# A two-part transformer kernel: the second part's norm becomes the head of its projection, the context's keys and values are made in the second layer's attention

## The reference, cut to what matters

```
for l in range(2):
    x = x + 0.5 * swiglu(rms_norm(x, norm_ffn1[l]), ffn1_in[l], ffn1_out[l])
    h = rms_norm(x, norm_mix[l]); proj = h @ w_in[l]
    ... o_a = rwkv7_mixer(...); o_b = diff_attention(...)
    x = x + merged @ w_out[l]
    x = x + 0.5 * swiglu(rms_norm(x, norm_ffn2[l]), ffn2_in[l], ffn2_out[l])
```

```
m  = silu(c) @ mod_w[l] + mod_b[l]            # sh1, sc1, g1, sh2, sc2, g2
h  = rms_norm(x, norm1_g[l]) * (1 + sc1) + sh1
mc = silu(c_ctx) @ mod_w[0] + mod_b[0]        # csh1, csc1 are used
hc = rms_norm(ctx, norm1_g[0]) * (1 + csc1) + csh1
q, k, v, ua, va = split(h @ w_in);  kc, vc = split(hc @ w_in[:, 512:768])
x = x + g1 * (concat(window_attention(q, k, v, kc, vc), chunk_gmlp(ua, va)) @ w_out)
x = x + g2 * peer_ffn(norm(x) ...)            # 8 heads x 16 experts for each token
```

## Time and profile before

| | us |
|---|---|
| three runs | 3255.67, 3258.58, 3261.69 |
| median | 3258.58 |
| profiled execution | 3255.88 |
| its span | 3253.7 |
| granted TensorE clock, mean of the span | 0.958 |

### The profile page before, as it was taken

How to read it: one execution, slowest core, us unless ns; L and a number is a source line. 1 busy time by engine, 2 the same in 40 slices (tenths; PEclk the granted TensorE clock), 3 DMA queues, 4 the chain that set the end, 5 groups by cost and what they waited for, 6 DMA issues and landing times. The chain is left out here.

```text
span 3253.7 us, 45326 instructions
## 1 busy us (share of the span) xinstructions
PE 2836.7 (87%) x16786; PEld 1877.1 (58%) x16786; DVE 2139.0 (66%) x3990; ACT 1311.9 (40%) x2973; POOL 581.2 (18%) x516
## 2 busy tenths in 40 slices
PE   7999988799999998879988999997778899777877
PEld 5877676578787877757856665432322555233332
DVE  5755766577575577657734577777775577777764
ACT  4433433344343353144422434444443335444443
POOL 0000000000000000000000025454444045444442
PEclk9999999999999999989987999999999999999999
DMA  7745201387584530137753369999999699999997
GB/s 271 267 165 177 87 3 41 142 276 261 195 276 175 180 113 3 41 112 255 276 200 142 103 275 426 427 426 427 427 427 427 236 418 427 427 427 427 427 427 314
DMA packets 252571, 858.38 MB, mean 264 GB/s; under 512 B 15031, under 2 KB 138807, under 8 KB 179517
## 3 DMA queue, kind: packets, MB, share of 16 engines
q0 software_dynamic: 73728, 536.90, 39.2%
q1 hardware_dynamic: 178622, 318.59, 27.9%
HBM read 847.05 MB, written 8.39 MB: 263 GB/s over the span
## 5 line engine op out<-in xcount | busy, mean ns | idle before, releaser
L3202 POOL DMA_INDIRECT raw_weights<-peer_rows,expert_ids x208 | 237.6, 1142 | 2247.4 <-DVE expert_ids L148 1966.0
L447 PE MATMUL banks<-weight_parts_hi,normedT_hi 128*128 128x512 f32 (+2 forms) x1152 | 458.9, 398 | 38.6 <-DVE weight_parts_lo L1147 12.0
L3312 PE MATMUL banks<-raw_weights,diagonals 128*128 128x512 f32 x832 | 409.6, 636 | 82.0 <-ACT diagonals L181 81.6
L449 PE MATMUL banks<-weight_parts_hi,normedT_lo 128*128 128x512 f32 (+2 forms) x1152 | 448.1, 389 | 0.0
L448 PE MATMUL banks<-weight_parts_lo,normedT_hi 128*128 128x512 f32 (+2 forms) x1152 | 447.9, 389 | 0.0
L3312 PE MATMUL banks<-query_weights,diagonals 128*128 128x512 f32 x704 | 335.9, 618 | 58.3 <-ACT diagonals L181 58.1
L3312 PEld LDWEIGHTS banks<-raw_weights,diagonals 128*128 128x128 f32 x832 | 158.6, 200 | 323.1 <-ACT diagonals L181 165.6
L157 DVE CUSTOM_DVE_ANT_0 modulation<-raw_weights,normed 128x1024 f32<-128x1024 f32 x208 | 255.0, 1226 | 129.3 <-DMA raw_weights<-peer_rows,expert_ids 118.3
L3312 PE MATMUL banks<-modulation,diagonals 128*128 128x512 f32 x512 | 248.6, 623 | 59.2 <-ACT diagonals L181 59.1
L181 ACT ACTIVATE gelu<-dots 128x1 f32<-128x1 f32 x512 | 102.0, 199 | 475.2 <-DVE dots L157 474.5
L157 DVE CUSTOM_DVE_ANT_0 modulation<-query_weights,normed 128x1024 f32<-128x1024 f32 x176 | 215.7, 1226 | 114.5 <-DMA query_weights<-peer_rows,expert_ids 104.9
(11 more groups left out here) (402 smaller groups left out, 4777.7 us busy)
## 6 DMA issues: line engine op xcount, KB each, us to landing
raw_weights<-ffn_in SPq DMA_DIRECT2D x88, 1024.0 KB, 7.5
side_weights<-mod_tiles SPq DMA_DIRECT2D x48, 1024.0 KB, 5.1
raw_weights<-ffn_out SPq DMA_DIRECT2D x44, 1024.0 KB, 6.1
raw_weights<-w_in SPq DMA_DIRECT2D x28, 1024.0 KB, 5.0
query_weights<-peer_w_q SPq DMA_DIRECT2D x16, 1024.0 KB, 10.8
raw_weights<-w_in SPq DMA_DIRECT2D x10, 1536.0 KB, 6.4
raw_weights<-w_branch SPq DMA_DIRECT2D x8, 1024.0 KB, 7.5
raw_weights<-w_out SPq DMA_DIRECT2D x8, 1024.0 KB, 6.3
```

What stands on the lines that cost most here:

```text
L447: nc.tensor.matmul(out, lhs.hi, rhs.hi, start=start, stop=False)
L449: return nc.tensor.matmul(out, lhs.lo, rhs.hi, start=False, stop=stop)
L3202: nc.gpsimd.indirect_dma_start(out=ring.rows(g), out_offset=None, in_=table, in_offset=bass.IndirectOffsetOnAxis(ap=ids[:, n, t:t + 1], ax ...
L3312: last = nc.tensor.matmul(k.bank(2 * j + half), diag[:, g % DIAGS, :], ring.rows(g)[:, D + half * BANK:D + (half + 1) * BANK], start=t == ...
```

## The change

What it does, part by part:

- **Start.** One stage `first_stage` in place of two: conditions first, then x in two halves, gains, only the first 512 columns of the constants, then the weights. ScalarE makes Silu and squares as each lands. The other constants load inside the first feed-forward stage, behind the second side load.
- **Side sums.** Each block's accumulator is loaded with a tile that holds the bias in its first row and zeros elsewhere; all eight products of a block are then multiply-adds. In layer 1 the order of blocks is changed so that those which the norm of the second part needs are ready after its first feed-forward, and its double blocks are 1 and 4 instead of 1 and 7.
- **Context.** `ContextKV` makes the context's keys and values in layer 1 of the first part: squares of the context at the end of the RWKV projection, the root beside the chunk work, then in `finish_mixers` 32 matmuls with two columns of ones that turn the partial sums into columns (4 behind each unit's values), gain and shift folded into columns, the product of the shift, and the product of context and weights; the keep-warm matmuls go. Values use bank 4 alone in this layer. The products are unsplit fp32. The result goes to DRAM.
- **Entry.** The two norm and modulation stages and the context's linear stage go. The projection's first two weight tiles load at the end of the last feed-forward stage, and the norm is the head of the projection (`ShiftedHead`). The partial sums, tables and context keys and values are loaded beside it, ahead of weight tile 2.
- **Row sums.** Eight row sums take the place of eight keep-warm matmuls in `window_mix`, with four copies on ScalarE and four on VectorE, and waits on them.
- **Expert layer.** No bias rows are loaded, no one-row matmuls made.

```diff
+def first_stage(k, a, lam, wts):
+            sp.dma_start(k.cond[:, :], a["cond_columns"]).then_inc(S["got"], 16)
+            for j in range(NT):
+                sp.dma_start(k.X[:, j, :], a["x"][0, j * P:(j + 1) * P, :]).then_inc(S[f"part_in{j}"], 16)
+            sp.dma_start(k.gains[:, :], a["gain_columns"]).then_inc(S["loaded"], 16)
+            sp.dma_start(k.C[:, 0:BANK], k.table_dram[:, 0:BANK]).then_inc(S["loaded"], 16)
+            preload(k, sp, wts)
+            sp.wait_ge(S["loaded"], 32)
...
@@ class SideSums
-    BOTH = (1, 7)
+    BOTH = ((1, 7), (1, 4))
+    def bias(self, sp, i):
+        if i >= 4:
+            sp.wait_ge(self.k.sem[f"side_out{u}"], self.stores(i - 4))
+        for who in range(2 if n in self.both else 1):
+            sp.dma_start(self.acc[:, u, who], self.biases[n]).then_inc(self.k.sem[f"part_in{u}"], 16)
...
         self.load(sp, i + 2)
+        if i >= 2 and i % 2 == 0:
+            self.bias(sp, i + 2)
...
-                if n % 2 == 0 and kc_ == 0:
-                    last = o.ts(acc, w, c, ALU.mult, free=True)
-                else:
-                    last = o.stt(acc, w, c, acc, ALU.mult, ALU.add, free=True)
+                last = o.stt(acc, w, c, acc, ALU.mult, ALU.add, free=True)
...
+class ShiftedHead(NormHead):
+    def act_copies(self, act, o, j, n):
+        act.wait_ge(self.k.sem["turned"], at + 1)
+        if at >= 2:
+            act.wait_ge(self.k.sem["copied_v"], at - 1)
+        for c, bank, _, _ in self.chunks(j, n):
+            last = o.fn(self.whole(n)[:, c % 2, :], bank, ACT.Identity, scale=self.gain(c), bias=self.shift(c), free=True)
+    def dve_lows(self, dve, o, j, n):
+        o.copy(hi, self.whole(n), free=True)
+        o.sub(lo, self.whole(n), hi.bitcast(F32)).then_inc(self.k.sem["copied_v"], 1)
...
@@ def swiglu
                 side.load(sp, 0)
+                side.bias(sp, 0)
+                side.bias(sp, 2)
                 sp.wait_ge(S["turned"], KC)
                 side.load(sp, 1)
+                for dst, src in extra:
+                    sp.dma_start(dst, src).then_inc(S["loaded"], 16)
...
@@ def finish_mixers
                 preload(k, sp, ahead)
+                if context is not None:
+                    context.sp(sp)
...
                         values(n - 1)
+                        if context is not None:
+                            context.pe_columns(pe, n - 1)
-                keep_warm(k, 0, 8)
+                if context is None:
+                    keep_warm(k, 0, 8)
+                else:
+                    context.pe_shift(pe)
+                    pe.wait_ge(S["grown"], 1)
+                    pe.wait_ge(S["stored"], N)
+                    for j in range(NT):
+                        context.pe_products(pe, j)
...
+                if context is not None:
+                    context.dve_columns(dve, o)
+                    context.dve_scale(o)
...
@@ class ContextKV
+    def pe_columns(self, pe, part):
+        if part == 0:
+            pe.wait_ge(k.sem["part_in0"], self.loaded)
+        for i in range(part * 4, part * 4 + 4):
+            who, c = divmod(i, 2 * KC)
+            last = k.nc.tensor.matmul(k.bank(5)[:, 2 * i:2 * i + 2], self.sums[:, who, c * P:(c + 1) * P], C("ones"),
+                                      start=True, stop=True)
+    def pe_shift(self, pe):
+        for c in range(KC):
+            last = k.nc.tensor.matmul(k.bank(6)[:, 0:2 * KVW], self.wide[:, c, :], self.w[:, c, :], start=c == 0, stop=c == KC - 1)
+    def pe_products(self, pe, j):
+        for c in range(KC):
+            last = k.nc.tensor.matmul(k.bank((4, 7)[j])[:, 0:2 * KVW], self.xT[:, c, j * P:(j + 1) * P], self.w[:, c, :],
+                                      start=c == 0, stop=c == KC - 1)
...
@@ def window_mix
-                keep_warm(k, 3, 6)
+                pe.wait_ge(S["got"], 1)
+                sums.pe(range(5))
+                pe.wait_ge(S["written"], 1)
+                sums.pe([5])
...
-                keep_warm(k, 3, 2)
+                pe.wait_ge(S["written"], 4)
+                sums.pe([6, 7])
                 pe.wait_ge(S["qk_out"], NT + 1)
+                pe.wait_ge(S["pre_done"], 2)
                 pair_logits(0)
+                pe.wait_ge(S["pre_done"], 4)
                 pair_logits(2)
...
@@ def attn_gmlp_layer
-            modulations(k, a, mods, ones, bias, cm, cx)
-            norm_pair_stage(k, [(cx, cx, cm[:, D:2 * D], cm[:, 0:D], cT), (k.X, h, mod[:, D:2 * D], mod[:, 0:D], hT)],
-                            a["norm1_g_2"][0:1, :], room.loads, w_ckv, RowSums(k, mod, ones, bias))
-            linear_stage(k, lambda c_, j: cT[:, c_, j * P:j * P + P], w_ckv, 2 * KVW,
-                         lambda o, t, j, bank: o.copy(kvc[:, j, :], bank, free=True), w_pr)
+        extra = [(to[:, blk * BANK:(blk + many) * BANK], a["mod_sums"][half][:, n * BANK:(n + many) * BANK])
+                 for to, (blk, half, n, many) in blocks] + room.loads + [(kvc[:, :, :], a["context_kv"])]
...
+                     head=ShiftedHead(k, k.folded[:, 1], hT, xn, rs), extra=extra)
```

More of the change, by code:

```diff
@@ L276, in _ @@
         def _(sp):
-            for dst, src in pairs:
-                sp.dma_start(dst, src).then_inc(k.sem["loaded"], 16)
-            if ahead is not None:
-                preload(k, sp, ahead)
-            sp.wait_ge(k.sem["loaded"], 16 * len(pairs))
+            sp.dma_start(k.cond[:, :], a["cond_columns"]).then_inc(S["got"], 16)
[5 more added lines that the diff above has]
+            sp.wait_ge(S["loaded"], 32)
+        @block.scalar
+        def _(act):
+            o = Ops(nc, act, False)
+            act.wait_ge(S["got"], 16)
+            o.fn(k.cond[:, :], k.cond[:, :], ACT.Silu)
+            for j in range(NT):
+                act.wait_ge(S[f"part_in{j}"], 16)
+                for half in range(2):
+                    o.fn(k.junk[:, :], k.X[:, j, half * BANK:(half + 1) * BANK], ACT.Square,
+                         total=k.squares[:, j, half:half + 1])
+        @block.vector
+        def _(dve):
+            for l in range(DEPTH):
+                init = 0.8 - 0.6 * math.exp(-0.3 * l)
+                nc.vector.memset(lam[:, l, 0:1], init)
+                nc.vector.memset(lam[:, l, 1:2], 1.0 - init)
     k.clear()
@@ L468, in _ @@
         def _(act):
+            if beside is not None:
+                beside.act_shift(act, Ops(nc, act, False))
             for n, (sources, dst) in enumerate(jobs):
@@ L478, in _ @@
                                         ALU.subtract).then_inc(low, 1)
+            if beside is not None:
+                beside.dve_finish(dve, Ops(nc, dve, True))
     k.clear()
@@ L904, in finish_steps, with linear_sum_stage @@
                 finish(o, t, j, k.bank(u * groups + j)[:, 0:width]).then_inc(drained, 1)
-        stream(k, block, wts, ahead, size, parts, summed, groups, finish_steps, head=head)
+        stream(k, block, wts, ahead, size, parts, summed, groups, finish_steps, head=head, extra=extra, act_end=act_end)
     k.clear()
-def linear_sum_stage(k, lhsT, kc, wts, finish, ahead=None, side=None, squares=False):
+def linear_sum_stage(k, lhsT, kc, wts, finish, ahead=None, side=None, squares=False, extra=()):
     nc = k.nc
@@ L957, in swiglu @@
+def swiglu(k, gain, w_in, w_out, ahead, side_part, extra=()):
     nc = k.nc
@@ L1454, in prepare, with rwkv @@
         k.clear()
-def rwkv(k, gain, w_proj, w_rest, proj, mu, w0, w2, a0, a2, g2, k_k, k_a, r_k, row_loads, columns, out, out_b, lamc, lam_now, ahead):
+def rwkv(k, gain, w_proj, w_rest, proj, mu, w0, w2, a0, a2, g2, k_k, k_a, r_k, row_loads, columns, out, out_b, lamc, lam_now, ahead,
+         context=None):
     nc = k.nc
@@ L1556, in act_squares @@
         act.wait_ge(S["reduced"], 1)
+        if self.other is not None:
+            o.fn(self.other[:, :, 0], self.other[:, :, 0], ACT.Sqrt, free=True)
         o.fn(self.ss[:, :, :], self.ss[:, :, :], ACT.Sqrt, free=True).then_inc(S["rooted"], 1)
@@ L1580, in dve_small @@
         if level == 4:
+            if self.other is not None:
+                o.add(self.other[:, :, 0], self.other[:, :, 0], self.other[:, :, 1], free=True)
+                o.ts(self.other[:, :, 0], self.other[:, :, 0], 1.0 / D, ALU.mult, EPS, ALU.add)
             dve.wait_ge(S["squared"], 1)
@@ L1584, in dve_small @@
             dve.wait_ge(S["rooted"], 1)
+            if self.other is not None:
+                o.recip(self.other[:, :, 0], self.other[:, :, 0], free=True)
             o.recip(self.ss[:, :, :], self.ss[:, :, :]).then_inc(S["drained"], 1)
@@ L1876, in rwkv_tiles, with finish_mixers @@
         k.clear()
-def finish_mixers(k, proj, y, qT, move, fresh, gained, rest, lam, gain_col, sub_gain, out, ahead):
+def finish_mixers(k, proj, y, qT, move, fresh, gained, rest, lam, gain_col, sub_gain, out, ahead, context):
     nc = k.nc
@@ L1888, in finish_mixers, with value_bank @@
     N = len(units)
+    def value_bank(n):
+        return 4 if context is not None else 4 + n % 2
```

(15 more changed lines are left out.)

376 lines of the change are left out of this document (159 added, 217 removed).

## The result

The changed kernel takes 3201.5 us (median of 4 runs, 3198.8 to 3208.6); the kernel before took 3258.4 beside it (4 runs, 3255.7 to 3261.7). The ratio is 0.983, 95% interval 0.982 to 0.985. The forecast was 3192, so the direction and most of the size came, and 10 us of the gain did not. Profile against profile it is -55.2 (3255.9 to 3200.4; spans 3253.7 and 3198.5) where the sum said -65.1.

The account below looks back on a forecast made before the run. Limits differ by stage (TensorE 87% busy on average), with the second part's entry a serial chain overlapping nothing; -67.9 + 0.4 - 8.7 + 0.7 + 10.4 = -65.1 gave 3192 us, 8-in-10 range 3181 to 3208.

Parts of the forecast that it names:

- Part 1: Second part's entry: modulation, pair-norm and context linear stages go, -67.9 us; tighter wait in the window stage, +0.4.
- three more tiles at 9.6: Entry projection: after the second tile's split at +22.4, three tiles of 9.6 us each end at +51.2.
- rival 1: Entry: 6.4 MB of other transfers move slower than 0.40 MB/us and delay weight tiles 2 and 3; 3200 us, chance 0.09.
- a sign of being wrong: Entry projection: a cast of the third or fourth tile waiting for its transfer would show the forecast wrong.
- Part 2: Kernel start: SP free at 9.1 and next stage open at 9.6 instead of 18.6; -8.7 us, bounds -6.2 to -9.0.
- The zero for the constants ahead of tile 2: First feed-forward stage: 1.1 MB of constants ahead of weight tile 2 cost 0 us, bounds 0 to 2.
- Part 3: Side sums from biases: dearer first products exceed Vector's slack by about 0.25 in three stages; +0.7 us, bounds 0 and 3.
- Part 4: Context keys and values beside the second layer's attention: stall, columns and tail products add 10.4 us, bounds +5 and +20.
- The tail's split, 4.1 + 8.2: End of second layer's attention: shift product 4.1 us, keys and values 8.2, at 0.5 per 256-column matmul.
- Rival 2: Second layer's attention tail: 24 products at half clock, 1.0 instead of 0.5 each, +12 less about 2; 3202 us, chance 0.15.
- sits without gaps: First part's feed-forward stages: the tensor engine was read as having no gaps, with VectorE close behind.
- gaps over 1 us: First-part feed-forward stages: TensorE gaps over 1 us would show the forecast wrong.

Follow-up runs that it names:

- the constants loaded whole: The changed kernel with the whole constants table (1.4 MB instead of 0.26) loaded ahead of the first weights again: 3205.6 us, ratio 0.985.
- the filled gap: The changed kernel with two or three keep-warm matmuls between first and second weight tile in the seven stages opening with a norm head: 3191.5 us, ratio 0.980.
- the cast taken out of the chain: The changed kernel with Scalar casting the second weight tile between the two token halves' copies in seven norm-head stages: 3184.5 us, ratio 0.979.
- the three orders: The changed kernel with context loads before branch weights, the second tile's cast earlier, and feed-forward weight tile 2 issued once tile 0 is split: 3164.5 us, ratio 0.972.
- plain first products: The changed kernel with each side block's first product plain again, bias tiles loaded but modulation biases left out of the result: 3201.8 us, ratio 0.984.

## Why the prediction was right, and where it fell short

**Part 1** (-67.9 + 0.4 forecast, -63.3 measured). Mechanism and order right, head right to 0.3, no coupling beyond what was summed; the window stage opened at +56.6 after the stage's opening instead of +52.2 (at 1736.5 where 1725.6 was forecast). The term that was mis-sized is "three more tiles at 9.6": the first of them took 12.6, since after TensorE's gap of 3.4 fifteen matmuls came at the half clock (15 x 0.17 = 2.5), and a tile took 9.85 where neighbouring casts of the earlier trace rows gave 9.6. The start of the second tile was 0.8 late, because its cast began at +16.0 and not +15.3. The transfer landed at +24.3 against the +22.8 forecast, and moving half of the others away gave nothing: rival 1 is refuted. But the third cast did wait for it, which the prediction had named as a sign of being wrong. That sign didn't fit its own sum, which has the tile land at +22.8, behind the end of tile 0 at +18.9 that the cast waits for in any case. The row sums cost 0.2.

**Part 2** (-8.7, measured -8.0). SP ended at 10.1 instead of 9.1, inside the bounds. That the transfers and not issuing hold it is shown by the constants loaded whole. The size is luck in part: 2.8 were summed for 1.1 MB, and the traces gave 1.8 between the kernel before and the changed one, 3.0 to 4.7 in the experiment. (The side chain of Silu and squares adds up to 7.7 and not 7.9; it ended at 8.1.) The zero for the constants ahead of tile 2 is right, even though Scalar's wait doubled (3.3 to 6.1).

**Part 3** (+0.7). The four stages measured +0.5, but spells of the clock move them by more than that. The dearer first product can't be told from nothing: with the plain one the later three stages agree to 0.3. What I had from the earlier trace rows for slack was enough.

**Part 4** (+10.4, measured 12.8 in its stages by the traces). TensorE's arrival was exact. The load came 1.7 late: I had 4.2 MB more at the 0.42 MB/us of the earlier trace rows, and they took 11.5 instead of 10. What I did not price is what follows a stall: the clock fell behind it, about 2.4 over the next three groups. The tail's split, 4.1 + 8.2, was 5.3 + 7.1: the first in good part at the half clock, the others (16 times 0.44) at the full one. Rival 2 came true only in small part: the products of keys and values ran at full clock, and the half clock came behind the stall and in the last columns, where I had not put it.

**The step that fell short** is one: durations at full clock behind a gap of TensorE of 2.5 to 4.4 us. I asked of every stall how long it was and never what the next matmuls would cost. It cost 2.5 in the entry, 2.4 in the attention and 1.7 in layer 2's projection, which the sum had at 0 (tile 10.1 instead of 8.4 behind a gap of 2.5; the kernel before had full clock there): 6.6 of the 10 us. The feed-forward stages are none of it, since the kernel before had as many slow matmuls there. The load's 1.7, the start's 0.7 and the entry's 1.5 of tile pitch and late second tile come to 3.9. Stages where nothing was forecast moved by -2.3 to +2.2, so a share of under 2 us can't be given to one cause.

One reading was wrong from the start: that TensorE "sits without gaps" in the feed-forward stages. It stood 3.0 us before the second tile in each of the four, in the kernel before too (the row at 41.93 above). The sign "gaps over 1 us" could therefore tell nothing, and the gap was the best lever in the program: the filled gap, the cast taken out of the chain and the three orders all work on it.

## What to carry to other kernels

Price a gap of the tensor engine twice: its length, and the matmuls behind it at half clock. Behind the gap of 3.0 us that was 0, 1.6 or 2.7 us in these two kernels, so give it a range and not a number. A stage that got longer is not yet slower for the change: look whether another one of its kind got shorter. Look for the chain that makes the gap before filling it: one cast moved into an idle stretch of its own engine and two loads issued in another order gave 37 us where the large change gave 57. A wait on a DMA says nothing until the engine that sets the pace is seen waiting too: of two here, Scalar's of 5.0 us was worth 0 and TensorE's of 4.4 us was worth 4.6 in its stage.

## Not expected of the hardware

Gaps of TensorE of 3.0 us in the same place were followed by full clock in one kernel and by 5.5 us at half clock in the other, and in stages of the same kind within one kernel by either. Filled with matmuls to 0.4 (feed-forward stages) and 0.8 (the others), none of the seven places showed a spell at the second tile. A stage that an edit does not touch can differ by 7 us between profiled runs: behind the same stall of 4.1 to 4.4 us the second layer's attention ran at half clock for 5 us in the changed kernel (stage 59.5) and for 17 in the one with plain first products (65.0; granted clock 0.55 from 1372 to 1391).

At the start 1.1 MB more in front of the weights delayed SP by 3.0 to 4.7 us. In the added 4.7 us the queue moved 383 GB/s, as it did elsewhere, that is 1.8 MB for 1.1 MB more in front. So the bytes ahead and the rate alone do not say when SP is released; what else does stays open.
